# One decoder layer on one core: the end of the merge stage, the y turns and the last stores are ordered anew

## The reference

```
mod = silu(c) @ ada_w + ada_b                      # six vectors: shift, scale, gate for each half
h = rms_norm(x, g0) * (1 + sc_m) + sh_m
proj = h @ w_in                                    # q, latent kv, indexer, z, conv input, dt, two gates
att = sparse attention (top 256 keys per query)    # eight heads of 128
y = chunked state-space scan, * silu(z), normalized per group of 512, * ssm_norm_g
merged = sigmoid(g_att) * (att @ w_o_att) + sigmoid(g_ssd) * (y @ w_o_ssd)
x = x + gt_m * rms_norm(merged @ w_out, g1)        # called x1 below
h = rms_norm(x, g2) * (1 + sc_f) + sh_f
x = x + gt_f * rms_norm(square(relu(h @ w_up)) @ w_down, g3)
```

## Time and profile before

| | us |
|---|---|
| median of 3 runs (2464.88 to 2469.07) | 2465.72 |
| the profiled execution | 2466.93 |
| its span, first to last instruction | 2465.2 |
| PE busy | 2343.8 |
| DVE busy | 1388.2 |
| POOL busy | 866.6 |
| ACT busy | 721.9 |

### The profile page before, as it was taken

The page is one execution under the profiler, slowest core; times in us unless marked ns, Lnnn a source line. Parts: engine busy times, 40 slices in busy tenths (PEclk is TensorE's granted clock), DMA queues, the critical chain, the costliest instruction groups (busy, mean ns, idle before and its releaser), DMA issues.

```text
span 2465.2 us, 31715 instructions
## 1 busy us (share of the span) xinstructions
PE 2343.8 (95%) x12022; PEld 1930.8 (78%) x12022; DVE 1388.2 (56%) x1963; ACT 721.9 (29%) x1360; POOL 866.6 (35%) x353
## 2 busy tenths in 40 slices
PE   3999999998999999999999999999899999999997
PEld 3977878875558988888877788898688888888885
DVE  4249999995667266675857466535332231322316
ACT  5144121106652335344364011025411211212112
POOL 1221233327772442726344223345223332233220
PEclk9999999999999999999999999999899999999999
DMA  7111342225561113131313343334111111111103
GB/s 268 35 35 45 145 178 102 93 70 172 189 194 49 51 41 129 56 128 44 137 48 133 137 171 125 114 106 149 54 52 52 49 36 51 51 51 41 44 34 137
DMA packets 145737, 233.92 MB, mean 95 GB/s; under 512 B 8068, under 2 KB 111844, under 8 KB 144612
## 3 DMA queue, kind: packets, MB, share of 16 engines
q1 hardware_dynamic: 121952, 173.45, 21.2%
q10 hardware_dynamic: 23684, 59.06, 6.2%
HBM read 180.06 MB, written 52.43 MB: 94 GB/s over the span
## 4 chain that ended last, share of the span: by engine, by line
PE 71%; issue 13%; DVE 11%; ACT 3%; DVEq 1%; DMA 1%; ACTq 0%
PE ps L647 69%; DVE score L1696 2%; DVE score L1758 1%; DVE top L1754 1%; DVE c_out L1866 1%; DVE probT L1791 1%; DVE mod_sum L1634 1%; PE ps L864 1%; DVEq L1748 1%; PE ps L963 0%; DVE x_tm L2038 0%; ACT decay L1491 0%; DMA x_d<-x_tm 0%; DVE x_tm L1975 0%; PE ps L896 0%
## 5 line engine op out<-in xcount | busy, mean ns | idle before, releaser
L647 PE MATMUL ps<-a_hi,w_hi 128*128 128x512 f32 x1728 | 679.7, 393 | 15.7 <-DVE a_lo L1624 4.5
L647 PE MATMUL ps<-a_lo,w_hi 128*128 128x512 f32 x1728 | 676.6, 392 | 0.0
L581 POOL CAST w_hi<-raw 128x2048 fp32r<-128x2048 f32 x90 | 177.1, 1968 | 1290.6 <-PE ps L647 1019.1
L647 PE MATMUL ps<-a_hi,w_lo 128*128 128x512 f32 x1728 | 546.2, 391 | 0.0
L583 POOL TENSOR_TENSOR w_lo<-raw,w_hi 128x2048 fp32r<-128x2048 f32 x90 | 434.0, 4822 | 7.2
L2000 DVE TENSOR_TENSOR x_tm<-x_tm,ps 128x1024 f32<-128x1024 f32 x120 | 146.5, 1221 | 453.2 <-PE ps L647 453.2
L647 PEld LDWEIGHTS ps<-a_hi,w_hi 128*128 128x128 f32 x1728 | 326.4, 189 | 86.2 <-DVE a_lo L1624 4.7
L647 PEld LDWEIGHTS ps<-a_hi,w_lo 128*128 128x128 f32 x1728 | 326.8, 189 | 68.7
L647 PEld LDWEIGHTS ps<-a_lo,w_hi 128*128 128x128 f32 x1728 | 326.7, 189 | 67.2
L647 PE MATMUL ps<-w_hi,a_hi 128*128 128x256 f32 (+1 forms) x896 | 259.6, 290 | 5.0 <-ACT row L1535 2.0
L647 PE MATMUL ps<-w_hi,a_lo 128*128 128x256 f32 (+1 forms) x896 | 253.5, 283 | 0.0
(11 more groups left out here) (254 smaller groups left out, 3096.4 us busy)
## 6 DMA issues: line engine op xcount, KB each, us to landing
raw<-in_w_in_dram SPq DMA_DIRECT2D x35, 1024.0 KB, 5.0
ada_raw<-in_ada_w_dram SPq DMA_DIRECT2D x16, 1024.0 KB, 8.6
raw<-in_w_up_dram SPq DMA_DIRECT2D x16, 1024.0 KB, 5.7
raw<-in_w_down_dram SPq DMA_DIRECT2D x16, 1024.0 KB, 4.7
gates<-gate_d SPq DMA_DIRECT2D x12, 1024.0 KB, 4.9
act_raw<-acts_d ACTq DMA_DIRECT2D x20, 512.0 KB, 6.3
ada<-in_ada_w_dram SPq DMA_DIRECT2D x8, 1024.0 KB, 20.7
acts_d<-decay ACTq DMA_DIRECT2D x16, 512.0 KB, 3.2
```

The lines of the kernel that those rows point to most:

```text
L581: nc.gpsimd.tensor_copy(hi, src).then_inc(hi_made, 1)
L647: return nc.tensor.matmul(o, a, b, start=start, stop=stop)
```

## The change

There are five edits. Two semaphores also become one (`vec_turned` and `seg_turned` are now `rows_turned`).

1. The four y turns stand inside the first output block, one ahead of each of k = 4 to 7; the wait for the last of their evacuations stands in the second block.
2. The drains of the merge stage go. The last of each four tokens raises `w_used` itself, and ACT waits on that instead.
3. The first half's turns stand after tokens 24 to 31, not 21 to 28. ACT and DVE have their parts of these in the matching places, three tiles of them between the second half's sums.
4. The first up block's first half takes the split tiles one at a time; it uses banks 0 and 2. Then comes the first half of the second up block (banks 1 and 3), three turns of the second half, the first block's second half (banks 4 and 5) with the other five turns between its steps, and the second block's second half.
5. x1 is stored to `out` instead of `x1_d`. Tiles 0 to 6 are scaled by DVE and added to what lies in `out` by a DMA on POOL's queue; only tile 7 is loaded back, added on DVE and stored by SP.

```
 # SP, tail
-            for t in range(4):
-                load_x1(t)
-            for t in range(NT):
-                sp.wait_ge(out_made, t + 1)
-                if t + 4 < NT:
-                    load_x1(t + 4)
-                sp.dma_start(out[0, t * P:(t + 1) * P, :], x_tm[:, t, :]).then_inc(out_stored, 16)
-            sp.wait_ge(out_stored, 16 * NT)
+            sp.dma_start(x_in[0][:, :], out[0, last * P:SEQ, :]).then_inc(res_in[0], 16)
+            sp.wait_ge(out_made, NT)
+            sp.dma_start(out[0, last * P:SEQ, :], x_tm[:, last, :]).then_inc(last_stored, 16)
...
 # POOL, behind the last split
+            for t in range(NT - 1):
+                pool.wait_ge(x_landed[t], 32)
+                pool.wait_ge(out_made, t + 1)
+                nc.gpsimd.dma_start(out[0, t * P:(t + 1) * P, :], x_tm[:, t, :], accum_op=ALU.add).then_inc(out_stored, 16)
...
 # PE, output block
-            out_block(N_O, 0, 0)
-            for f in range(4):
-                y_turn(NG - 1, f)
-            pe.wait_ge(yt_out, NG * 4)
+            out_block(N_O, 0, 0, late=lambda k, m: y_turn(NG - 1, k - 4) if m == 0 and k >= 4 else None)
+            pe.wait_ge(yt_out, NG * 4 - 1)
             pe.wait_ge(gate_used, 1)
-            for j in range(1, 4):
+            out_block(N_O + 1, 1, 0, late=lambda k, m: pe.wait_ge(yt_out, NG * 4) if (k, m) == (0, 1) else None)
+            for j in range(2, 4):
                 out_block(N_O + j, j, 0)
...
 # PE, merge stage
-                tm_token(n, t, ps[:, v % 6, 0:WC], WC).then_inc(merge_done, 1)
-                if v % 4 == 3:
-                    pe.drain().then_inc(w_used[n % 2], 1)
-                if 21 <= v < 29:
-                    norm_turn(1, (v - 21,), banks=(6, 7))
+                tm_token(n, t, ps[:, v % 6, 0:WC], WC).then_inc(merge_done if v % 4 < 3 else w_used[n % 2], 1)
+                if v >= 24:
+                    norm_turn(1, (v - 24,), banks=(6, 7))
...
             w_wait(N_MLP)
-            pe.wait_ge(h_split, 3 * KT)
             pe.wait_ge(merge_out, 31)
-            up_half(N_MLP, 0).then_inc(up_half_done, 1)
+            up_half(N_MLP, 0, 0, ready=2 * KT).then_inc(up_half_done, 1)
             pe.wait_ge(merge_out, 32)
-            norm_turn(1, range(KT, 2 * KT))
-            pe.wait_ge(h_split, 4 * KT)
-            up_half(N_MLP, 1).then_inc(w_used[N_MLP % 2], 1)
             w_wait(N_MLP + 1)
-            for q in range(2):
-                pe.wait_ge(up_out, 2 * q + 2)
-                last = up_half(N_MLP + 1, q)
-            last.then_inc(w_used[(N_MLP + 1) % 2], 1)
+            up_half(N_MLP + 1, 1, 0)
+            norm_turn(1, (KT, KT + 1, KT + 2), banks=(6, 7))
+            up_half(N_MLP, 0, 1, ready=3 * KT, turned=lambda k: norm_turn(1, (KT + 3 + k,), banks=(6, 7)) if k < 5 else None
+                    ).then_inc(w_used[N_MLP % 2], 1)
+            pe.wait_ge(up_out, 2)
+            up_half(N_MLP + 1, 1, 1).then_inc(w_used[(N_MLP + 1) % 2], 1)
...
 # ACT, merge stage, in the loop over i behind the tokens
                         merge_evac(16 * g + 13 + i)
+                        if g:
+                            norm_evac(1, 24, (5 + i,), banks=(6, 7))
...
-                        act.dma_start(x1_d[u * P:(u + 1) * P, :], x_tm[:, u, :]).then_inc(x_landed[u], 16)
+                        act.dma_start(out[0, u * P:(u + 1) * P, :], x_tm[:, u, :]).then_inc(x_landed[u], 16)
...
 # DVE, merge stage
-                    norm_split(1, range(KT))
+                    norm_split(1, range(5))
                 for i in range(7):
...
+                    if g and i < 3:
+                        norm_split(1, (5 + i,))
...
 # DVE, tail
-                    V.link(ve.scalar_tensor_tensor(x_tm[:, u, :], x_tm[:, u, :], stat[:, 56 + u:57 + u], row[1][:, :], ALU.mult, ALU.mult))
-                    dve.wait_ge(res_in[u % 4], 16 * (u // 4 + 3))
-                    ve.tensor_tensor(x_tm[:, u, :], x_tm[:, u, :], x_in[u % 4][:, :], ALU.add).then_inc(out_made, 1)
+                    ins = ve.scalar_tensor_tensor(x_tm[:, u, :], x_tm[:, u, :], stat[:, 56 + u:57 + u], row[1][:, :], ALU.mult, ALU.mult)
+                    if u == NT - 1:
+                        V.link(ins)
+                        dve.wait_ge(res_in[0], 16 * 3)
+                        ins = ve.tensor_tensor(x_tm[:, u, :], x_tm[:, u, :], x_in[0][:, :], ALU.add)
+                    ins.then_inc(out_made, 1)
```

More of the change, by code:

```diff
@@ L250, in hybrid_block @@
     acts_d = nc.dram_tensor("acts_d", (3 * KT, P, SEQ), F32, kind="Internal").ap()
-    x1_d = nc.dram_tensor("x1_d", (SEQ, D), F32, kind="Internal").ap()
     ctx = ExitStack()
@@ L367, in hybrid_block @@
         FIRST_OUT = (5, 0, 1, 2)
+        FIRST_UP = ((0, 4, 2, 5), (1, 0, 3, 2))
         STEPS = 2 * NT
@@ L528, in _ @@
             load_down(N_ALL - 1, NC - 1)
+            last = NT - 1
             sp.wait_ge(w_used[0], N_ALL // 2)
-            def load_x1(t):
-                sp.wait_ge(x_landed[t], 32)
-                sp.dma_start(x_in[t % 4][:, :], x1_d[t * P:(t + 1) * P, :]).then_inc(res_in[t % 4], 16)
-            for t in range(4):
-                load_x1(t)
-            for t in range(NT):
-                sp.wait_ge(out_made, t + 1)
-                if t + 4 < NT:
-                    load_x1(t + 4)
-                sp.dma_start(out[0, t * P:(t + 1) * P, :], x_tm[:, t, :]).then_inc(out_stored, 16)
-            sp.wait_ge(out_stored, 16 * NT)
+            sp.wait_ge(x_landed[last], 32)
+            sp.dma_start(x_in[0][:, :], out[0, last * P:SEQ, :]).then_inc(res_in[0], 16)
+            sp.wait_ge(out_made, NT)
+            sp.dma_start(out[0, last * P:SEQ, :], x_tm[:, last, :]).then_inc(last_stored, 16)
+            for t in range(NT):
+                sp.wait_ge(x_landed[t], 32)
+            sp.wait_ge(out_stored, 16 * last)
+            sp.wait_ge(last_stored, 16)
         @block.gpsimd
@@ L647, in mm, with fm_block @@
                 return nc.tensor.matmul(o, a, b, start=start, stop=stop)
-            def fm_block(n, group, extra=0, act_ready=None, act_used=None, banks=None):
+            def fm_block(n, group, extra=0, act_ready=None, act_used=None, banks=None, late=None):
                 s = n % 2
@@ L657, in fm_block @@
                     for m in range(2):
+                        if late is not None:
+                            late(k, m)
                         wh = w_tile(w_hi, s, k, m * P, m * P + P)
@@ L1058, in _, with out_block @@
                         fill(g, *divmod(part, 2))
-            def out_block(n, j, o, turn=None):
+            def out_block(n, j, o, turn=None, late=None):
                 def at_turn(v, per):
@@ L1069, in out_block @@
                 last = fm_block(n, j % 2, extra=0 if turn is None else turn * 2, act_ready=ready, act_used=used,
-                                banks=FIRST_OUT if (o, j) == (0, 0) else None)
+                                banks=FIRST_OUT if (o, j) == (0, 0) else None, late=late)
                 last.then_inc(w_used[n % 2], 1)
@@ L1099, in _ @@
             for t in range(4):
-                tm_token(N_OUT, t, ps[:, t, 0:WC], WC, ks=range(KT - 2, KT)).then_inc(merge_done, 1)
-            pe.drain().then_inc(w_used[N_OUT % 2], 1)
+                tm_token(N_OUT, t, ps[:, t, 0:WC], WC, ks=range(KT - 2, KT)).then_inc(merge_done if t < 3 else w_used[N_OUT % 2], 1)
             pe.wait_ge(gate_used, 48)
@@ L1539, in merge_evac @@
                 t, j = v // 16 * 4 + v % 4, v // 4 % 4
-                act.wait_ge(merge_done, v + 1)
+                if v % 4 < 3:
+                    act.wait_ge(merge_done, v // 4 * 3 + v % 4 + 1)
+                else:
+                    n = N_OUT + v // 4
+                    act.wait_ge(w_used[n % 2], n // 2 + 1)
                 nc.scalar.activation(sq[:, 0:WC], ps[:, v % 6, 0:WC], ACT.Square,
@@ L1549, in _ @@
                     merge_evac(v)
-                    if v >= 21:
-                        norm_evac(1, 24, (v - 21,), banks=(6, 7))
+                    if v >= 24:
+                        norm_evac(1, 24, (v - 24,), banks=(6, 7))
                 for i in range(8):
@@ L1574, in _, with hidden @@
                         nc.scalar.activation(x_tm[:, u, :], x_tm[:, u, :], ACT.Copy, scale=stat[:, 40 + u:41 + u]).then_inc(normed, 1)
-            norm_evac(1, 24, range(KT, 2 * KT))
-            def hidden(n, c, b, extra=0, first=False):
+            norm_evac(1, 24, range(KT, 2 * KT), banks=(6, 7))
+            def hidden(n, c, b, extra=0, first=False, banks=range(4)):
                 if first:
@@ L1590, in hidden @@
                     m, q = divmod(j, 2)
-                    nc.scalar.activation(u_tmp[j][:, :], ps[:, j, :], ACT.Relu).then_inc(up_out, 1)
+                    nc.scalar.activation(u_tmp[j][:, :], ps[:, banks[j], :], ACT.Relu).then_inc(up_out, 1)
                     act.wait_ge(up_out, c * 4 + (i + 1))
@@ L1595, in hidden @@
```

(6 more changed lines are left out.)

19 lines of the change are left out of this document (11 added, 8 removed).

## The result

The changed kernel takes 2445.53 us at the median of 4 runs (2445.20 to 2448.12), the kernel before 2465.72 (4 runs, 2464.88 to 2469.07): a ratio of 0.9915 with a 95% interval of [0.9903, 0.9927]. So it is faster by some 20 us, where 24.7 were forecast. The forecast of 2441 is missed by 4.5: the time lies 0.5 above the forecast's own range (2437 to 2445) and inside the wide one (2436 to 2456).

The account below looks back on a forecast made before the run. PE, busy 95% of the span, was taken as the bound, with DVE bounding the tail. Gains 1.5 + 2.5 + 13.7 + 7.0 = 24.7 us, from the 2465.72 median, gave 2441; own range 2437 to 2445, wide range 2436 to 2456.

Parts of the forecast that it names:

- The two up blocks: From T, the end of token 31 with its drain, to the first down matmul: 64.6 us becomes 50.9, so 13.7 gained.
- tile 7's `a_lo`: In the first up block's first half, PE was to wait 0.9 us (0 to 3) for tile 7's split on DVE.
- the first turned tile: In the up blocks, PE was to wait 1.4 us for it to pass ACT twice and DVE once.
- `normed`: Second half's scaled input, due at T + 22.4, PE there at T + 23.2; 0.8 us of wait taken (0 to 5).
- the third rival: The last `x1` tile's store lands in 8.45 us, `normed` comes 4 later, PE waits: 2446; chance 0.15.
- The tail: End of the kernel: seven DVE additions go, PE bounds again, the end comes at 2458.2; 7.0 us gained.
- the last plain store and the end took 3.0: Tail step: after DVE's last addition at 2454.5, 3.0 us as before, so the plain chain ends at 2457.5.
- The drains: Merge stage: 0.5 us each; three ahead of token 15 (1.5) and those after 23 and 27 (1.0), 2.5 gained.
- The y turns: First output block: 1.8 us of slow clock saved, start 0.3 later; 1.5 gained (0.3 lost to 3 gained).
- Cost what they save: Rival on the output block's y turns: they gain nothing, 2442.5, inside the forecast's own range; no chance given.
- the signs that the prediction named as right: No pause between tokens 3 and 4, 5.6 us idle before token 22, k = 4 wait then full clock, 50 to 52 from token 31, 2.80 sums.
- those named as wrong: Hole over 3 us after two first halves, slow first up block second half, chain ending in POOL's DMA, output block past 1368.

## Why the prediction came out as it did

- *The two up blocks, 13.7.* Right in its mechanism: 50.9 from T to the first down matmul, as worked out; 1.1 for tile 7's `a_lo` (0.9 taken; its terms, 7.3, 2.5 and 1.1, add to 0.2 less than was written), 1.2 for the first turned tile (1.4), though the third turn waits there for its bank, and not a matmul for the split. The scaling beside POOL took 5.20 (5.13 in the earlier trace rows). That the sum fits to 0.1 is luck in part: for `normed` there was no wait (0.8 taken), and nearly as much went where nothing was taken, into the first matmuls and turns behind the two waits (1.69 and 1.38 for six matmuls in the chain). The late `normed` of the third rival, at 2446, hits the time measured by accident only.
- *The tail, 7.0.* The term that failed, with 4.8. DVE's and PE's part is right (2.80 apart, 6.9 from the last sum to the addition's end). The step that failed is "the last plain store and the end took 3.0": in the kernel before this store ran alone (landed in 2.6), here beside adds, which I had let land late without asking what they take from it. It took 5.3, and 5.8 to the end; without the adds it is 2.6 again. The adds themselves took 5.4 at the median, below the twice 3.9 that I allowed; the last (6.2 from its issue at 2435.59) landed about 1.2 ahead of the plain store, where I had it last. The Trainium skill ("Collectives: The Full Stack", the bandwidth ceiling: the fold count) has the adding step of a ring of cores at half the rate of its copying step, because it reads two sources. The trace agrees for these adds, with some 190 GB/s at full DMA engines against 391 for the plain store. I had used this rule for the adds' landing, from which 0.7 more would have come, and not for the load on the engines. The other rule of the Trainium skill ("SBUF — State Buffer", who interferes with whom) shows nothing here: POOL's issue of tile 6's add takes 0.86 and starts at 2435.59, 0.5 after the scaling's end.
- *The drains, 2.5.* Three drains ahead of token 15 are worth 1.3 (1.5 forecast). The 1.0 behind it is not there: the slow clock behind the wait takes 2.9 (11.46 for three tokens, against 8.6), where the prediction kept the 1.8 of before. The idle time ahead of token 22 is 4.8 (5.6 forecast), released by ACT's copies, as the text said.
- *The y turns, 1.5.* The step itself came out at 1.3: the wait for the scaling at k = 4, the start 0.3 later, and the slow clock gone in the next block. Two things failed. That the turns behind the block cost 1.8 at the slow clock was read from one profile: with the same 2.8 us wait the clock was full in one of three. And what was gained is not kept: in C the clock takes 1.5, in a place where neither the text nor any rival looked; whether the turns' place does that stays open. "Cost what they save" had the right sum.

So of 24.7, 2.2 are missing in the tail, 1.5 in tokens 0 and 1, some 1.2 behind the drains and 0.2 in the turns: 5.1, with 2.1 gained where nothing was forecast (1.05 ahead of the change, 1.07 in the `x1` store): 21.7. All the signs that the prediction named as right came, and none of those named as wrong; none of them looked at the plain store beside the adds or at the clock of tokens 0 and 1.

## What to carry to other kernels

Work that doesn't depend on a late result belongs between its request and its use: half a weight block put there was the main part of 13.8 us, and ACT's four copies paid 7.6. A new kind of DMA is to be priced by what it takes from the transfers beside it, not by its own landing alone: seven adds cost the plain store behind them 2.7. Where a change is worth 1 or 2 us, read it between two fixed events of the trace: the stretch ahead of the change varied by more.

## What was not expected of the hardware

- The same 2.0 us wait of PE for `row` was followed by full clock in some profiles (40.59 for 336 matmuls) and by a granted clock of 0.57 to 0.67 over the next 4 us in others (42.07), that is mostly 1.2 GHz: full in 5 of 12. By the place of the y turns 260 us earlier it was full in 3 of 3 (behind the block), 1 of 8 (from k = 4) and 1 of 1 (from k = 5). With the wait at 1.1 us the clock was up in both profiles that have it. The cause is open.
- Seven adding stores of 512 KB, issued 2.8 us apart (the last 1.6), kept the DMA engines 90% busy or more for some 20 us at about 190 GB/s, and made a plain store beside them take 5.3 for 2.6.
